# A hybrid attention/SSD/MoE block: the last gathers of expert rows without addition in the DMA, the addition on DVE

## Chip, cores and metric

One core of a Trainium2 chip runs the whole program. The metric is device time in microseconds, from the program's start to its end; lower is better. Beside it stands the span, from the first to the last instruction of a profiled execution.

## What is computed

One layer of a streaming encoder with 512 tokens of width 1024, in float32. What matters here is its last part:

```python
h1 = layernorm(alpha * h + mix)                       # mix: attention and SSD branches
moe = hier_moe(h1)                                    # 32 experts, 2 for each token, D_FF 256
ple = sigmoid(h1 @ w_ple_gate + b) * (p @ w_ple)
out = layernorm(alpha * h1 + moe + ple)
```

Each token picks one of 4 groups and in it 2 of 8 experts. An expert computes `silu(t @ w_gate) * (t @ w_up)`, weighted, times `w_down`. So the expert part of a token is the sum of two rows of 1024 numbers, one from each of its experts.

## The kernel before

**Tiling.** The 512 tokens are NT = 4 tiles of 128 partitions. The residual `alpha * h1 + ple` stands in SBUF as `base[:, i, :]`, one 128x1024 tile for each i, and is complete before the expert pairs begin (`s_base_ready` counts its 16 parts, all written by DVE). SBUF is one large array in two parts: the `ring` of 12 slots of 2048 words per partition, which holds weights, and the `arena` for all else. All code of a queue is written out by hand, one block for each engine: `sp` (weight loads), `pool` (GpSimd), `pe` (TensorE), `act` (ScalarE), `dve` (VectorE). Each engine works through its own list in order; semaphores tie the lists together.

**Experts.** The 32 experts run as PAIRS = 16 pairs, with room for CAP = 64 tokens for each expert, so a pair has 128 rows. Pair p uses the slots 6 (p mod 2) to 6 (p mod 2) + 5 of the ring: gate, up and down of the first expert, then of the second. For each pair TensorE multiplies gate and up (L1119, signal `s_gu_mm`), ACT takes the tanh (L1413), DVE forms the product in two instructions (L1981 and L1984 or L1986, in `hidden`), TensorE transposes it (L1144), multiplies down (L1134), and the 128x1024 result is copied out of PSUM in two halves, one by ACT and one by DVE (L2012, in `out_half`), into `eout`.

**Pairs 0 to 14.** POOL stores the rows of each pair by an indirect DMA (L754) to the tensor `y_rows` in HBM, which has a row for each place of each expert. Rows that no token takes are skipped. The semaphores `y_st[0]` and `y_st[1]` count the stores.

**The gathers.** Behind the 15 stores, POOL waits for both `y_st` and then issues eight indirect DMAs (L764). Gather (c, i) fetches for each token of tile i the row of its c-th choice (`rowsU`), and adds it to `base[:, i, :]` in the DMA (`compute_op=ALU.add`). All c = 0 come first, then c = 1; the gather (1, i) waits for the landing of (0, i), since both change the same tile. `y_gath[i]` counts the landings.

**Extra pairs.** Experts with over 64 tokens get extra pairs. Their number is known only at run time: each engine loads it from the tensor `ctl` (`value_load`, L2030 on DVE, L1449 on ACT) and runs a loop of MORE_PAIRS = 8 rounds with a branch in each (L2031 and L2032 on DVE, L1450 on ACT). In this data the number is zero, so the rounds do nothing.

**The last pair.** Pair 15 isn't stored. After the loop, TensorE combines its rows into each tile by a matmul with the matrix `last_rowsT`, tile by tile (L1157, in `combine`, 4 matmul records for each tile), to two PSUM banks that tiles i and i + 2 share: tiles 2 and 3 wait for `s_last_added`. Its input is `eout`, of which ACT and DVE copied a half each. DVE then waits for `y_gath[i]` = 32 and adds the banks to `base` (L2005, in `added`).

**The tail.** ACT takes the LayerNorm statistics of tiles 0 and 1, DVE those of tiles 2 and 3 (L1514 and L1515, in `tile_stats`), each behind the add of its tile. DVE then forms the roots for all tiles (L1519 to L1521), normalizes tiles 0 to 2 (L1523, L1524); ACT and POOL (L694, L695, `last_normed`) normalize tile 3; four DMAs write the output.

DVE's list around the change is, in order: `hidden(14)`, the row weights of the last pair (L1991 to L1999), `out_half` of pair 14, `hidden(15)`, the load and the loop, `out_half` of pair 15, then for each tile the wait, the add and the statistics.

Of the kernel before, what the change touches and what calls it, by code (L numbers as in the profile page):

```python
# [17 lines left out]
ALU = mybir.AluOpType  # L18
# [7 lines left out]
P = 128  # L26
D = 1024
S = 512
NT = S // P
# [211 lines left out]
def block_kernel(nc, aps, out):  # L241
    with ExitStack() as ctx:
# [154 lines left out]
        s_av_read = sem("av_read")  # L397
        s_ah1_ready = sem("ah1_ready")
        s_base_ready = sem("base_ready")
        s_bple_in = sem("bple_in")  # L400
        s_cb_act = sem("cb_act")
        s_cb_dve = sem("cb_dve")
# [99 lines left out]
        s_w_lo = sem("w_lo")  # L502
        s_wdt_split = sem("wdt_split")
        s_hT_hi = sem("hT_hi")
        s_wple_in = sem("wple_in")
        s_wsmall_in = sem("wsmall_in")
        s_xT_mm = sem("xT_mm")
        s_xdec_ready = sem("xdec_ready")
# [10 lines left out]
        s_yo_read = sem("yo_read")  # L519
        s_ys_read = sem("ys_read")  # L520
        s_z_read = sem("z_read")
        s_zero_set = sem("zero_set")
        s_zeroed = sem("zeroed")
        sems = {x.name: x for x in (
            s_av_read, s_dtT_read, s_cb_act, s_cb_dve, s_conv_read, s_dt_read, s_g_read, s_h1T_read, s_h_ready, s_hT_read, s_xgT_sb,
# [43 lines left out]
        def expert_slot_in(eng, former, parity, half, w):  # L569

            s = expert_slot(parity, half, w)
            eng.wait_ge(slot_in[s], former * 16 + 16 * (landings(s, len(loads) - 1) + 1))

        block = ctx.enter_context(nc.Block())

# [2 lines left out]
        def _(sp):  # L578
# [49 lines left out]
            sp.wait_ge(s_ys_read, KD)  # L628
            gate_slice(0)
            sp.wait_ge(s_pe_mix, 2 * NT)  # L630
            sp.dma_start(wple, aps["w_ple"][0].rearrange("(k p) n -> p k n", p=P)).then_inc(s_wple_in, 16)
            experts(0)
            sp.wait_ge(s_pe_pl, NT)
            gate_slice(2)
# [7 lines left out]
            with sp.Fori(0, MORE_PAIRS) as j:  # L642
                with sp.If(pairs > j):
                    sp.wait_ge(s_y_mm, j + LAST)
                    for half in range(2):
                        e = sp.value_load(ctl[0:1, bass.ds(j * 2 + half, 1)], min_val=0, max_val=NE - 1)
                        for w, t in ((0, wg), (1, wu)):
                            src = t[bass.ds(e, 1)].rearrange("a (p k) f -> p (a k) f", p=P)
                            slot = expert_slot(0, half, w)
                            sp.dma_start(ring[:, slot], src).then_inc(slot_in[slot], 16)  # L650
                        src = wd[bass.ds(e, 1)].rearrange("a (p k) n -> p (a k) n", p=P)
                        slot = expert_slot(0, half, 2)
                        sp.dma_start(ringN[:, slot], src).then_inc(slot_in[slot], 16)
                sp.nop()
# [3 lines left out]
        def _(pool):  # L658
# [26 lines left out]

            zt = shaped(R_Y, "p (r n) -> p r n", r=2, n=D)
            pool.wait_ge(s_dist_in, 1)
            g.memset(zt, 0.0).then_inc(s_zero_set, 1)
            pool.wait_ge(s_zero_set, 1)

            def last_normed(x, w, b, norms):

# [63 lines left out]
                    in_offset=None, bounds_check=ROWS - 1, oob_is_err=False).then_inc(y_st[p % 2], 16)  # L756
            for parity in range(2):
                pool.wait_ge(y_st[parity], 16 * (PAIRS // 2 - parity))
            pool.wait_ge(s_base_ready, 4 * NT)
            for c in range(2):  # L760
                for i in range(NT):
                    if c:
                        pool.wait_ge(y_gath[i], 16)
                    g.indirect_dma_start(  # L764
                        out=base[:, i, :], out_offset=None, in_=y_dram,
                        in_offset=bass.IndirectOffsetOnAxis(ap=rowsU[:, 2 * i + c:2 * i + c + 1], axis=0),
                        bounds_check=ROWS - 1, oob_is_err=True, compute_op=ALU.add).then_inc(y_gath[i], 16)
            pool.wait_ge(s_ln_in, 64)
            last_normed(base[:, NT - 1, :], A1w, A1b, 1)

# [2 lines left out]
        def _(pe):  # L773
# [289 lines left out]
            route(logits, NT - 1).then_inc(s_pe_rt, 1)  # L1063


            pe.wait_ge(s_wple_in, 16)
            pe.wait_ge(s_pT_read, 2)
            for n in range(4 * NT):
                s, i = divmod(n, NT)
# [406 lines left out]
        def _(dve):  # L1476
# [524 lines left out]
            def added(i, made, signal):  # L2001
# [3 lines left out]
                v.tensor_tensor(base[:, i, :], base[:, i, :], psum[:, b0:b0 + 2, :].rearrange("p b n -> p (b n)"), ALU.add)\  # L2005
                    .then_inc(signal, 1)

            def out_half(made, stores, u, signal):
                dve.wait_ge(*made)
                if not (isinstance(stores, int) and stores == 0):  # L2010
                    dve.wait_ge(y_st[u % 2], stores)
                v.tensor_copy(eout[:, u % 2, 512:1024], psum[:, 5, :]).then_inc(signal, 1)  # L2012

            dve.wait_ge(s_w_row, 16 * 2 * NT + 16)
            for p in range(PAIRS):
# [11 lines left out]
                    v.tensor_copy(rv[11], rv[8]).then_inc(s_more_added, 1)  # L2027
                out_half((s_y_mm, p + 1), 16 * q, p % 2, s_y_dve)

            pairs = dve.value_load(ctl[0:1, EXTRA + 1:EXTRA + 2], min_val=0, max_val=MORE_PAIRS)  # L2030
            with dve.Fori(0, MORE_PAIRS) as j:  # L2031
                with dve.If(pairs > j):  # L2032
                    dve.wait_ge(s_more_added, j * 4 + 1)
                    dve.wait_ge(s_rowf_moved, j + PAIRS // 2)
                    rows_weighted(more_rows, 0, j * 2 + 2, s_more_rows)
                    dve.wait_ge(s_more_rows, j * 3 + 1)
                    tokens_rows(j + PAIRS // 2, 0, j * 4 + 2 * PAIRS, j + PAIRS // 2, 2 * CAP)
                    hidden(j + PAIRS, 0)
                    out_half((s_y_mm, j + LAST + 1), 16 * (PAIRS // 2), 0, s_y_dve)
                    for i in range(NT):  # L2040
                        dve.wait_ge(y_gath[i], 32)
                        added(i, (s_more_mm, j * 4 + i + 1), s_more_added)
                dve.nop()

            out_half((s_last_y, 1), 16 * (LAST // 2), LAST % 2, s_last_y)
            for i in range(NT):
                dve.wait_ge(y_gath[i], 32)
                added(i, (s_last_mm, i + 1), s_last_added)
                if i >= 2:
                    dve.wait_ge(s_last_added, i + 1)  # L2050
                    tile_stats(base[:, i, :], i)
# [29 lines left out]
```

## Time and profile before

| | |
|---|---|
| median of 3 runs | 848.09 us (846.92 to 849.23) |
| the profiled execution: its own time | 849.05 us |
| its span, first to last instruction | 847.3 us |
| TensorE busy | 796.1 us, 94% of the span |
| DVE, ACT, POOL busy | 431.7, 176.2, 160.6 us |
| HBM read, written | 147.12 MB, 22.56 MB |
| mean granted TensorE clock | 0.981 of full |

All rows are of one profiled execution, in us from the span's start. A timeline row reads: start, duration, engine, line, operation, output from input, count, and in brackets the idle time of the engine ahead of it and what ended it. A chain row reads: start, duration, what; a DMA in it runs from its issue to the semaphore that released the next step. PEld is TensorE's weight load. A name with q (DVEq) is the sequencer of an engine, whose instructions (loads of a register, branches) count as no busy time.

### The profile page before, as it was taken

To read this page: it belongs to the slowest core of one execution; us is meant where nothing else is said; L and a number is where in the kernel's file an instruction comes from. 1 tells how busy PE (TensorE), PEld (TensorE's weight loads), DVE (VectorE), ACT (ScalarE), POOL (GpSimd) and SP (SyncE) were. 2 spreads that over 40 slices of the span, in tenths; PEclk is the share of its full clock that TensorE was granted. 3 is DMA by queue.
4 is the path that set the end of the run, shared out by engine and by line. 5 is a ranking of instruction groups with operands and counts; after the bars stand their busy time and mean duration, and the time that the engine had idled before them with its cause. 6 is when DMAs were issued, how large, how long until landed. Compare 5 with 4: busy or idle time off the path is not lost.

```text
span 847.3 us, 10153 instructions
## 1 busy us (share of the span) xinstructions
PE 796.1 (94%) x4045; PEld 534.1 (63%) x4045; DVE 431.7 (51%) x765; ACT 176.2 (21%) x327; POOL 160.6 (19%) x101
## 2 busy tenths in 40 slices
PE   5999999999999999999999999999999999998753
PEld 2987789998878787444444788884545454554221
DVE  6698765767688885112147579262313222301217
ACT  4213325553322230000000200221112111111012
POOL 4924760000323221000000344000000000000052
PEclk9999999999999999999999989999999999999886
DMA  9796331111311224613100631906999999999693
GB/s 302 294 368 143 100 98 52 51 51 51 98 51 51 50 51 142 255 50 100 50 0 1 261 137 51 347 1 268 420 422 421 421 420 424 419 422 423 286 178 120
DMA packets 58920, 166.25 MB, mean 196 GB/s; under 512 B 15813, under 2 KB 38495, under 8 KB 45050
## 3 DMA queue, kind: packets, MB, share of 16 engines
q1 hardware_dynamic: 51748, 139.69, 43.6%
q0 software_dynamic: 6432, 23.77, 8.8%
q10 hardware_dynamic: 694, 2.14, 0.6%
q8 instruction: 33, 0.54, 0.3%
q14 instruction: 13, 0.11, 0.0%
HBM read 147.12 MB, written 22.56 MB: 200 GB/s over the span
## 4 chain that ended last, share of the span: by engine, by line
PE 79%; DMA 11%; DVE 7%; issue 1%; ACT 1%; POOL 1%; SPq 0%; DVEq 0%; POOLq 0%
PE psum L806 24%; PE psum L1119 11%; PE psum L1034 7%; PE psum L1024 6%; PE psum L1073 5%; DMA ring<-in_w_exp_up_dram 5%; PE psum L1134 5%; PE psum L1015 3%; PE psum L1096 3%; PE psum L1097 3%; DMA ring<-in_w_in_dram 3%; DMA arena<-y_rows,rowsU 2%; PE psum L964 2%; PE psum L984 1%; PE psum L1075 1%; PE psum L914 1%
## 5 line engine op out<-in xcount | busy, mean ns | idle before, releaser
L806 PE MATMUL psum<-ring_r 128*128 128x512 f32 (+1 forms) x832 | 214.1, 345 | 4.6 <-DVE arena_r L1533 1.7
L806 PEld LDWEIGHTS psum<-ring_r 128*128 128x128 f32 x832 | 145.1, 191 | 25.7 <-issue 4.4
L1234 ACT COPY arena<-psum 128x256 f32<-128x256 f32 (+4 forms) x104 | 58.4, 579 | 288.2 <-PE psum L1041 139.8
L1119 PE MATMUL psum<-ring,arena 128*64 128x512 f32 x512 | 112.8, 593 | 4.0 <-DMA ring<-in_w_exp_up_dram 3.2
L701 POOL TENSOR_TENSOR ring_r<-ring,ring_r 128x2048 fp32r<-128x2048 f32 x16 | 73.9, 4622 | 204.8 <-ACT ring_r L1234 204.8
L806 PE MATMUL psum<-arena_r,ring_r 128*128 128x512 f32 (+1 forms) x288 | 106.0, 368 | 0.0
L1119 PEld LDWEIGHTS psum<-ring,arena 128*64 128x64 f32 x512 | 38.1, 137 | 76.0 <-issue 75.0
L1981 DVE SCALAR_TENSOR_TENSOR arena<-arena,psum 128x256 f32<-128x256 f32 x16 | 10.0, 624 | 111.3 <-ACT arena L1413 111.3
L1096 PE MATMUL psum<-arena_r 128*128 128x256 f32 x256 | 65.3, 293 | 0.0
L1134 PE MATMUL psum<-ring,arena 128*64 128x512 f32 x256 | 62.2, 631 | 1.6 <-issue 1.6
L754 POOL DMA_INDIRECT y_rows<-arena,storeU x15 | 14.6, 975 | 258.7 <-DVE arena L2012 258.7
L1097 PE MATMUL psum<-arena_r 128*128 128x256 f32 x256 | 62.4, 282 | 0.0
L806 PEld LDWEIGHTS psum<-arena_r,ring_r 128*128 128x128 f32 x288 | 55.1, 191 | 8.3
L1073 PE MATMUL psum<-arena 128*128 128x256 f32 x256 | 59.3, 386 | 0.0
L1034 PE MATMUL psum<-ring,arena 128*128 128x512 f32 x128 | 55.2, 593 | 1.6 <-DVE arena L1801 1.6
L1096 PEld LDWEIGHTS psum<-arena_r 128*128 128x128 f32 x256 | 48.8, 191 | 11.4 <-issue 11.4
L1024 PE MATMUL psum<-arena,ring 128*128 128x512 f32 x128 | 55.1, 592 | 0.0
L1073 PEld LDWEIGHTS psum<-arena 128*128 128x128 f32 x256 | 49.5, 194 | 6.9
L2012 DVE COPY arena<-psum 128x512 f32<-128x512 f32 x16 | 11.1, 692 | 79.0 <-PE psum L1134 79.0
L1097 PEld LDWEIGHTS psum<-arena_r 128*128 128x128 f32 x256 | 48.9, 191 | 0.0
L1034 PEld LDWEIGHTS psum<-ring,arena 128*128 128x128 f32 x128 | 24.2, 190 | 32.5 <-issue 30.1
L1024 PEld LDWEIGHTS psum<-arena,ring 128*128 128x128 f32 x128 | 24.3, 190 | 30.6 <-issue 30.6
(265 smaller groups left out, 1004.6 us busy)
## 6 DMA issues: line engine op xcount, KB each, us to landing
ring<-in_w_exp_gate_dram SPq DMA_DIRECT2D x32, 1024.0 KB, 11.6
ring<-in_w_exp_up_dram SPq DMA_DIRECT2D x32, 1024.0 KB, 15.6
ring<-in_w_exp_down_dram SPq DMA_DIRECT2D x32, 1024.0 KB, 16.2
ring<-in_w_in_dram SPq DMA_DIRECT2D x18, 1024.0 KB, 5.3
y_rows<-arena POOLq DMA_DIRECT2D x12, 1024.0 KB, 16.9
ring<-in_w_out_ssd_dram SPq DMA_DIRECT2D x4, 1024.0 KB, 7.2
ring<-in_w_out_dram SPq DMA_DIRECT2D x4, 1024.0 KB, 18.5
arena<-in_w_ple_gate_dram SPq DMA_DIRECT2D x4, 1024.0 KB, 7.9
```

The source lines that it names most:

```text
L701: g.tensor_tensor(lo, ring[:, SLOT_OF[seq]], hi.bitcast(F32), ALU.subtract).then_inc(s_w_lo, 1)
L806: t = mm(o, a, b, start=(first and j == 0), stop=(last and j == 2))
L964: t = mm(o[:, m * P:(m + 1) * P], dta[:, c, hh:hh + 1].broadcast_to([P, P]), upper, start=True, stop=True)
L1015: t = mm(o, ringN[:, s, j % 2, n * P:(n + 1) * P], yaT[:, j, :], start=(j == 0), stop=(j == 3))
L1024: t = mm(o, ringN[:, s, k % 2, n * P:(n + 1) * P], yT[:, :, k, :], start=(k == 0), stop=(k == KD - 1))
L1034: t = mm(o, mixT[:, k, i * P:(i + 1) * P], ringN[:, s, k % 2, b * 512:(b + 1) * 512], start=(k == 0), stop=(k == KD - 1))
L1073: mm(o[:, 0:PS], h1T[:, i, k, :], pgw[s % 2][:, k, :], start=(k == 0), stop=(k == KD - 1))
L1096: mm(o, h_hi[i][:, k, :], onehot[q % 2][:, i, 0:width], start=(i == 0), stop=False)
L1097: t = mm(o, h_lo[:, i, k, :], onehot[q % 2][:, i, 0:width], start=False, stop=(i == NT - 1))
L1119: t = mm(psum[sides[half], parity, :], xgT[buf][:, k, c:c + CAP], ring[:, s:s + 2, k, :], start=(k == 0), stop=(k == KD - 1))
L1134: t = mm(psum[sides[half], 4 + b, :], eactT[:, parity, k, sides[half]], ringN[:, s, k, b * 512:(b + 1) * 512], start=(k == 0), stop=(k == 1))
L1234: return nc.scalar.copy(dst, src)
```

## The change

The eight gathers drop the addition. Gather (c, i) writes to a free place of the ring, `back(i, c)`: half a slot for each tile, slots 0 and 1 for c = 0, slots 6 and 7 for c = 1. DVE adds it to `base[:, i, :]` by an instruction of its own (`back_added`, signal `s_back_added`): the four of c = 0 behind `hidden(15)` and ahead of the load and the loop over extra pairs, those of c = 1 behind the loop and `out_half`, each ahead of the add of its tile. POOL no longer waits for `s_base_ready` (DVE does); ahead of the gathers of c = 1 it waits for `s_gu_mm` = 16, as pair 15's gate and up are read from slots 6 and 7. Each gather (1, i) still waits for the landing of (0, i). In the loop over extra pairs, SP and DVE wait for the four adds. Two semaphores are dropped to make room: the load of `w_ple` is counted with other small loads, and the zeroing of a tile with POOL's own steps.

```diff
--- before.py
+++ after.py
@@ -397,6 +397,7 @@
         s_av_read = sem("av_read")
         s_ah1_ready = sem("ah1_ready")
         s_base_ready = sem("base_ready")
+        s_back_added = sem("back_added")
         s_bple_in = sem("bple_in")
         s_cb_act = sem("cb_act")
         s_cb_dve = sem("cb_dve")
@@ -502,7 +503,6 @@
         s_w_lo = sem("w_lo")
         s_wdt_split = sem("wdt_split")
         s_hT_hi = sem("hT_hi")
-        s_wple_in = sem("wple_in")
         s_wsmall_in = sem("wsmall_in")
         s_xT_mm = sem("xT_mm")
         s_xdec_ready = sem("xdec_ready")
@@ -519,7 +519,6 @@
         s_yo_read = sem("yo_read")
         s_ys_read = sem("ys_read")
         s_z_read = sem("z_read")
-        s_zero_set = sem("zero_set")
         s_zeroed = sem("zeroed")
         sems = {x.name: x for x in (
             s_av_read, s_dtT_read, s_cb_act, s_cb_dve, s_conv_read, s_dt_read, s_g_read, s_h1T_read, s_h_ready, s_hT_read, s_xgT_sb,
@@ -570,6 +569,10 @@
 
             s = expert_slot(parity, half, w)
             eng.wait_ge(slot_in[s], former * 16 + 16 * (landings(s, len(loads) - 1) + 1))
+
+        def back(i, c):
+
+            return ringN[:, 6 * c + i // 2, i % 2, :]
 
         block = ctx.enter_context(nc.Block())
 
@@ -628,7 +631,7 @@
             sp.wait_ge(s_ys_read, KD)
             gate_slice(0)
             sp.wait_ge(s_pe_mix, 2 * NT)
-            sp.dma_start(wple, aps["w_ple"][0].rearrange("(k p) n -> p k n", p=P)).then_inc(s_wple_in, 16)
+            sp.dma_start(wple, aps["w_ple"][0].rearrange("(k p) n -> p k n", p=P)).then_inc(s_wsmall_in, 16)
             experts(0)
             sp.wait_ge(s_pe_pl, NT)
             gate_slice(2)
@@ -642,6 +645,7 @@
             with sp.Fori(0, MORE_PAIRS) as j:
                 with sp.If(pairs > j):
                     sp.wait_ge(s_y_mm, j + LAST)
+                    sp.wait_ge(s_back_added, NT)
                     for half in range(2):
                         e = sp.value_load(ctl[0:1, bass.ds(j * 2 + half, 1)], min_val=0, max_val=NE - 1)
                         for w, t in ((0, wg), (1, wu)):
@@ -685,8 +689,7 @@
 
             zt = shaped(R_Y, "p (r n) -> p r n", r=2, n=D)
             pool.wait_ge(s_dist_in, 1)
-            g.memset(zt, 0.0).then_inc(s_zero_set, 1)
-            pool.wait_ge(s_zero_set, 1)
+            link(g.memset(zt, 0.0))
 
             def last_normed(x, w, b, norms):
 
@@ -756,15 +759,16 @@
                     in_offset=None, bounds_check=ROWS - 1, oob_is_err=False).then_inc(y_st[p % 2], 16)
             for parity in range(2):
                 pool.wait_ge(y_st[parity], 16 * (PAIRS // 2 - parity))
-            pool.wait_ge(s_base_ready, 4 * NT)
             for c in range(2):
+                if c:
+                    pool.wait_ge(s_gu_mm, PAIRS)
                 for i in range(NT):
                     if c:
                         pool.wait_ge(y_gath[i], 16)
                     g.indirect_dma_start(
-                        out=base[:, i, :], out_offset=None, in_=y_dram,
+                        out=back(i, c), out_offset=None, in_=y_dram,
                         in_offset=bass.IndirectOffsetOnAxis(ap=rowsU[:, 2 * i + c:2 * i + c + 1], axis=0),
-                        bounds_check=ROWS - 1, oob_is_err=True, compute_op=ALU.add).then_inc(y_gath[i], 16)
+                        bounds_check=ROWS - 1, oob_is_err=True).then_inc(y_gath[i], 16)
             pool.wait_ge(s_ln_in, 64)
             last_normed(base[:, NT - 1, :], A1w, A1b, 1)
 
@@ -1063,7 +1067,7 @@
             route(logits, NT - 1).then_inc(s_pe_rt, 1)
 
 
-            pe.wait_ge(s_wple_in, 16)
+            pe.wait_ge(s_wsmall_in, 16 * 4)
             pe.wait_ge(s_pT_read, 2)
             for n in range(4 * NT):
                 s, i = divmod(n, NT)
@@ -2005,6 +2009,13 @@
                 v.tensor_tensor(base[:, i, :], base[:, i, :], psum[:, b0:b0 + 2, :].rearrange("p b n -> p (b n)"), ALU.add)\
                     .then_inc(signal, 1)
 
+            def back_added(i, c):
+
+                dve.wait_ge(y_gath[i], 16 * c + 16)
+                if c:
+                    dve.wait_ge(s_back_added, i + 1)
+                v.tensor_tensor(base[:, i, :], base[:, i, :], back(i, c), ALU.add).then_inc(s_back_added, 1)
+
             def out_half(made, stores, u, signal):
                 dve.wait_ge(*made)
                 if not (isinstance(stores, int) and stores == 0):
@@ -2027,6 +2038,9 @@
                     v.tensor_copy(rv[11], rv[8]).then_inc(s_more_added, 1)
                 out_half((s_y_mm, p + 1), 16 * q, p % 2, s_y_dve)
 
+            dve.wait_ge(s_base_ready, 4 * NT)
+            for i in range(NT):
+                back_added(i, 0)
             pairs = dve.value_load(ctl[0:1, EXTRA + 1:EXTRA + 2], min_val=0, max_val=MORE_PAIRS)
             with dve.Fori(0, MORE_PAIRS) as j:
                 with dve.If(pairs > j):
@@ -2037,14 +2051,15 @@
                     tokens_rows(j + PAIRS // 2, 0, j * 4 + 2 * PAIRS, j + PAIRS // 2, 2 * CAP)
                     hidden(j + PAIRS, 0)
                     out_half((s_y_mm, j + LAST + 1), 16 * (PAIRS // 2), 0, s_y_dve)
+                    dve.wait_ge(s_back_added, NT)
                     for i in range(NT):
-                        dve.wait_ge(y_gath[i], 32)
                         added(i, (s_more_mm, j * 4 + i + 1), s_more_added)
                 dve.nop()
 
             out_half((s_last_y, 1), 16 * (LAST // 2), LAST % 2, s_last_y)
             for i in range(NT):
-                dve.wait_ge(y_gath[i], 32)
+                back_added(i, 1)
+                dve.wait_ge(s_back_added, NT + 1 + i)
                 added(i, (s_last_mm, i + 1), s_last_added)
                 if i >= 2:
                     dve.wait_ge(s_last_added, i + 1)
```

## Rows read from the trace of the kernel before

**Rows 1.** The page, its head, part 1 and part 5.

```profile
span 847.3 us, 10153 instructions
...
PE 796.1 (94%) x4045; PEld 534.1 (63%) x4045; DVE 431.7 (51%) x765; ACT 176.2 (21%) x327; POOL 160.6 (19%) x101
...
L1134 PE MATMUL psum<-ring,arena 128*64 128x512 f32 x256 | 62.2, 631 | 1.6 <-issue 1.6
```

**Rows 2.** The chain of waits, the last 50 us: start, us, what.

```profile
800.46 3.22 DMA y_rows<-arena,storeU
...
806.49 1.58 POOL arena L764
...
808.38 9.44 DMA arena<-y_rows,rowsU
...
818.56 9.20 DMA arena<-y_rows,rowsU
...
833.46 0.22 DVE arena L1515
```

**Rows 3.** Windows: length, busy time of each engine, then PEclk, DMA share, GB/s.

```profile
720.00:740.00 20.00, 20.00 (x109) 9.38 (x106) 5.62 (x8) 2.81 (x6) 1.38 (x2) 1.00 1.02 422
800.00:804.00 4.00, 4.00 (x22) 1.40 (x20) 0.00 (x0) 0.00 (x0) 0.97 (x1) 1.00 0.21 80
816.00:820.00 4.00, 3.22 (x9) 1.44 (x8) 0.69 (x1) 0.59 (x1) 1.44 (x1) 1.00 1.06 211
824.00:828.00 4.00, 3.90 (x6) 1.55 (x6) 1.48 (x3) 3.83 (x9) 0.00 (x0) 0.58 1.04 206
```

**Rows 4.** The timeline of the last 44 us, all engines.

```profile
804.50 1.68 POOL L764 DMA_INDIRECT arena<-y_rows,rowsU  x1 [3.07 <-DMA y_rows<-arena,storeU]
...
806.85 0.60 DVE L1986 TENSOR_TENSOR arena<-arena,psum 128x256 f32<-128x256 f32 x1
...
810.25 1.57 POOL L764 DMA_INDIRECT arena<-y_rows,rowsU  x1 [0.30 <-issue]
...
816.07 0.69 DVE L2012 COPY arena<-psum 128x512 f32<-128x512 f32 x1 [8.63 <-PE psum L1134]
...
816.82 3.70 PE L1157 MATMUL psum<-arena 128*128 128x512 f32 x8 [0.78 <-DVE arena L2012]
...
824.10 5.40 PE L1157 MATMUL psum<-arena 128*128 128x512 f32 x8 [3.58 <-DVE arena L2005]
...
829.05 1.42 DVE L1514 BATCH_NORM_STATS2 arena<-arena 128x6 f32<-128x512 f32 x2
...
830.75 1.22 DVE L2005 TENSOR_TENSOR arena<-arena,psum 128x1024 f32<-128x1024 f32 x1
...
832.00 1.42 DVE L1514 BATCH_NORM_STATS2 arena<-arena 128x6 f32<-128x512 f32 x2
```

**Rows 5.** Lines of the load and the loop, on DVE and ACT: ns min/median/max, starts.

```profile
L2030 DVEq TENSOR_LOAD <-ctl x1: 1740/1740/1740, 806.9 to 806.9; - x1
...
L2031 DVEq COMPARE_BRANCH  x8: 50/56/72, 809.8 to 814.7; - x8
...
L1449 ACTq TENSOR_LOAD <-ctl x1: 478/478/478, 805.8 to 805.8; - x1
...
L1450 ACTq COMPARE_BRANCH  x8: 40/45/55, 807.0 to 810.0; - x8
```

**Rows 6.** The timeline of POOL and of DVE, indirect stores beside adds.

```profile
518.45 1.81 POOL L743 DMA_INDIRECT row_weights<-arena,rowsU  x1 [0.30 <-issue]
520.56 0.98 POOL L743 DMA_INDIRECT row_weights<-arena,rowsU  x1 [0.30 <-issue]
521.85 0.98 POOL L743 DMA_INDIRECT row_weights<-arena,rowsU  x1 [0.30 <-issue]
...
518.18 1.23 DVE L1949 TENSOR_TENSOR arena_r<-arena 128x1024 fp32r<-128x1024 f32 x1
...
520.57 1.24 DVE L1952 TENSOR_TENSOR arena_r<-arena_r,arena 128x1024 fp32r<-128x1024 f32 x1
```

## The prediction

> **What bounds the kernel now.** I read the page's first part, then the chain of waits for the last 50 us, then the timeline of that stretch, the sources of a few lines and windows. TensorE is busy 94% of the span [rows 1], but the change touches nothing ahead of the last pair, and there the chain has left TensorE: the store of pair 14's rows, then gathers, then DVE [rows 2]. The store is released 3.22 us after its issue; the two longest links are gathers of 9.44 and 9.20 us; DVE ends its work on the last tile at 833.67, and what follows (roots, norms, output) takes 13.6 us and is not touched. The eight adding gathers keep all 16 DMA engines busy at 211 GB/s, where weight loads get 422 GB/s at the same share [rows 3]: an adding gather costs twice the engine time of its bytes, 524 KB / 211 = 2.5 us each, 20 us in all. So now the tail is bound by the DMA engines. One thing more lies in it, which matters below. Between its last work on pair 15 (the product issued at 806.85) and the copy of its output half at 816.07 [rows 4], DVE loads the number of extra pairs and runs the empty loop over them: the load starts at 806.9 and takes 1.74 us, the last branch is at 814.7 [rows 5]. The half copy came 1.3 us after that, so today the loop hides behind pair 15 on TensorE and ACT, with 1.3 us to spare.
>
> **The change, part by part.**
> *Gathers made plain.* With no addition in the DMA I expect the rate of a plain transfer, 524/422 = 1.24 us each. The trace has no plain gather of rows; its issue on POOL is bounded by the indirect stores of weights (0.98 us, start to start 1.29 [rows 6]) and by the adding gathers (1.57, and 1.89 from the start at 806.49 to that at 808.38 [rows 2]). I take 1.29: the stores are the only plain form, and the adding one has to read its target as well. The first gather stays at 804.50, since its wait (both parities of stores) is unchanged. The fourth then starts at 804.50 + 3 x 1.29 = 808.4. Landing: the store moved 80 GB/s x 4 us = 320 KB [rows 3] in 3.22 us; the gather moves 204 KB more, 0.5 us, so 3.7 us, and the fourth lands at **812.1**. The second four are issued at 809.7 to 813.5, their new wait (TensorE done with pair 15's gate and up) already over, since ACT has taken up that result before its own load at 805.8 [rows 5]; all land by 817.5. Where DVE's part below is right, nobody waits for them.
>
> *The second four, added on DVE.* Four more instructions of 128x1024 with both inputs in SBUF, 1.22 to 1.24 us [rows 6].
>
> *The first four, added on DVE ahead of the loop.* This is the term that decides. They stand behind the product of 806.85 and before the load. In the time from 807.45 to 816.07 DVE has 8.6 us without work, so 4 x 1.25 = 5 us look free; but the engine's queue is in order, and the load and the loop now start only when the fourth add is issued, which waits for the fourth gather. From the issue of the instruction ahead of the load to the end of the loop took 814.75 - 806.85 = 7.9 us, and some 0.05 us more to the next instruction. Whether the load waits for the instruction ahead to end isn't shown: that add is 0.6 us longer than the product of now. I take 0.25 of it. So the half copy comes at 812.1 + 7.95 + 0.25 = **820.3** in place of 816.07. TensorE's combination of the last pair needs both halves of that output, and waits with it; behind it in DVE's queue stands the whole list of the tail.
>
> *From the half copy to the end of the statistics.* Now: 833.67 - 816.07 = 17.6 us, of which much is waiting for gathers. After: copy and start of TensorE 0.75; the combination of tile 0, 1.85 us at the full clock (8 matmuls in 3.70) or 2.4 at half (824.10 and on) [rows 4]. TensorE will have been idle for 4.9 us; in the trace its granted clock was 0.58 of full in the window 824 to 828 [rows 3], after 3.58 us without work [rows 4], so I take 2.4, less than an even half because part of it ran at full. DVE's add of tile 0's gathered rows hides beside it. Then the add of tile 0 from PSUM 1.25, three tiles of two adds each 3 x 2.5 = 7.5, and two statistics of 1.68 (829.05 to 830.75, and 832.00 to 833.67) 3.35. Sum 0.75 + 2.4 + 1.25 + 7.5 + 3.35 = 15.25, against 17.6. TensorE's later combinations (tile 2 after the add of tile 0) stay ahead of DVE, and so do ACT's statistics of two tiles, which start with the adds of tiles 0 and 1, and TensorE's rows for the last norm, behind its combination of tile 3.
>
> *The rest costs nothing.* The two dropped semaphores wait for the same events; POOL's wait for the finished residual goes to DVE, which wrote it itself ahead of the expert pairs; SP's new wait stands in the loop over extra pairs, which is empty (L1134, the down matmuls, ran 256 times, 16 for each of 16 pairs [rows 1]). POOL's list behind the gathers (last norm) waits for ACT as now. Slots 0, 1, 6 and 7 of the ring are read by nobody after pair 15's gate and up.
>
> **Sum.** 820.3 + 15.25 = 835.55, against 833.67: +1.9 us. The gain of 2.35 us in the second stretch is more than paid for by 4.2 us of delay ahead of it. The profiled execution took 849.05 (span 847.3), the median is 848.09; the difference is put on the median: **850.0 us**, +0.2%. A measurement of this kernel can tell about 0.3% (2.5 us) from no change, so the forecast is "within".
>
> **A rule against the trace.** On contention between the new adds and POOL: in rows 6 an issue that began at 518.45 beside a two-input DVE instruction took 1.81 us in place of 0.98, while the next, which began together with another such, took 0.98, and the DVE instructions kept their 1.22 to 1.24. If each of the last four issues lost 0.83, the last would land near 820.8, and DVE asks for it after 830: no effect. The Trainium skill (SBUF — State Buffer, "SBUF: two separate sides") says that DVE and GpSimd share a port pair as an exclusive lock, held for a whole instruction, taken by a DVE instruction with two SBUF inputs only against a GpSimd instruction that reads SBUF. That rule would speak against the change if the lock worked the other way too: the rival E.
>
> For the landing, the Trainium skill (DMA: Bandwidth & Descriptors, "Anatomy of one DMA — SWDGE (gpsimd) path") gives a fit of 2.0 us and bytes over 436 GB/s, an estimate of 3.2 us for this gather. By it the sum would be +1.4; my 3.7 is the trace's store lengthened.
>
> **The rivals.**
> A, the forecast: 850.0, itself between +1.1 (clock full, load not waiting) and +3.0 (load waits for the whole add, a straggling engine lands the gather 0.7 later).
> B, slower: the plain gathers keep POOL for 1.57 us. The fourth is then issued at 810.25 as now and lands 0.6 us later after its issue: 814.55, the half copy is at 822.8, and the end moves by +4.4: 852.5. It passes the bound of 0.3% once the fourth gather lands after 812.7, that is from a spacing of about 1.45 us. For it: the duration could belong to the gather's direction, not to the addition. Against: the plain stores at 0.98.
> C, the load or the loop is shorter when moved. ACT's load took 0.48 beside DVE's 1.74, and its loop ends at 810.1 after 3.5 us beside DVE's 5.8 [rows 5]. Should the load have been held by POOL's issue (which ended at 808.07 [rows 2], the load at 808.6), it may be 1.2 shorter; then 848.5. With the loop at ACT's pace instead, 847.7; with both, 846.2.
> D, faster: the half copy isn't delayed at all (the load and loop run ahead of the waiting adds, or finish by 816). Then the clock has no idle stretch to fall in, 816.07 + 14.7 = 830.8, -2.9 us: 845.2. It is the most the change can give, as DVE's own list of 14.7 us then bounds; and it needs a landing by 808, against the 3.7 us.
> E, POOL's issue holds up the fourth add by up to 0.98 us: +2.9, 851.0. In rows 6 no DVE instruction did that.
>
> **How the numbers follow.** A 0.57, of which 0.15 lies over the bound of 2.5 us (landing and load both late); B 0.25; C 0.10; D 0.05; E 0.03. Faster 0.05 (D); within 0.42 + 0.10 = 0.52; slower 0.15 + 0.25 + 0.03 = 0.43. The range leaves out D and the end of C below, and the upper part of B: 847.3 to 852.9.
>
> **What would show it.** Right: DMA engines free between gathers, at no more than 1.3 us of full rate each; gathers 1.3 us apart; a wait of DVE for the fourth gather till about 812; the load's start at 812.1 and the loop's last branch at 820; the half copy at 820.3 with "issue" before it; TensorE's combination waiting for it since 816; no wait of DVE for a gather after that. Wrong: a half copy at 816 (then D), gathers 1.9 apart (B), a load of 0.5 us (C), or a wait in DVE's last list for a landing of the second four.

## The result

The changed kernel took **852.40 us** in the median of 8 runs (848.81 to 854.62), the kernel before 847.73 in 8 runs (846.03 to 849.23). The ratio is 1.0051 with a 95% interval of 1.003 to 1.0072. That is slower by half a per cent, 4.3 us by the ratio. The same two kernels on another chip gave 1.0053 (1.0031 to 1.0076).

The profiled executions hide this: the span after is 847.7 us beside 847.3 before. The one that was profiled after is also among the quickest of its kernel (849.49 beside the median of 852.40). What hides the rest lies ahead of the changed code: this execution came to the last pair's row weights 2.3 us earlier (786.62 in place of 788.93), and in the windows from 788 to 796 us its granted clock was 0.66 and 0.91 of full, where that of before was 0.82 and 0.50. So gate and up of pair 15, the last thing that both kernels do alike, ended at 805.75 before and at 802.28 after. From there on the stretches can be compared. The end of DVE's statistics came 27.9 us later before (833.67) and 31.9 us later after (834.15), so the tail is 3.9 us longer. The two ends of gate and up, and in the kernel before ACT's half copy, which began together with DVE's:

```profile
798.72 7.03 PE L1119 MATMUL psum<-ring,arena 128*64 128x512 f32 x32
...
816.07 0.59 ACT L1234 COPY arena<-psum 128x512 f32<-128x512 f32 x1 [5.59 <-PE psum L1134]
```

```profile
795.68 6.60 PE L1123 MATMUL psum<-ring,arena 128*64 128x512 f32 x30
```

First the chain of waits of the changed kernel (start, us, what), from the fourth gather to the first add from PSUM. L768 is the gather (L764 before), L2017 the add of gathered rows, L2044 to L2046 the load and the loop (L2030 to L2032), L2023 the half copy (L2012), L1161 the combination (L1157), L2009 the add from PSUM (L2005).

```profile
805.09 5.67 DMA ring<-y_rows,rowsU
...
810.78 0.56 DVE arena L2017
...
811.37 0.21 DVEq L2044
...
817.33 0.05 DVEq L2045
...
817.49 0.70 DVE arena L2023
...
818.24 6.29 PE psum L1161 x8
```

The chain of before [rows 2] had nothing of DVE's sequencer in it; now 5.7 us of the tail (from the loop's first move at 811.69 to its last branch at 817.33) are an empty loop, and the 0.9 us ahead of it, from the issue of the fourth add at 810.78, are the load. The timeline of the same stretch shows both sides of it:

```profile
801.03 1.09 POOL L768 DMA_INDIRECT ring<-y_rows,rowsU  x1 [3.06 <-DMA y_rows<-arena,storeU]
...
803.38 0.60 DVE L1990 TENSOR_TENSOR arena<-arena,psum 128x256 f32<-128x256 f32 x1
...
805.09 1.01 POOL L768 DMA_INDIRECT ring<-y_rows,rowsU  x1 [0.30 <-issue]
...
805.48 1.22 DVE L2017 TENSOR_TENSOR arena<-arena,ring 128x1024 f32<-128x1024 f32 x1 [1.50 <-DMA ring<-y_rows,rowsU]
...
810.78 1.23 DVE L2017 TENSOR_TENSOR arena<-arena,ring 128x1024 f32<-128x1024 f32 x1 [0.19 <-DMA ring<-y_rows,rowsU]
...
813.86 0.58 ACT L1238 COPY arena<-psum 128x512 f32<-128x512 f32 x1 [6.85 <-PE psum L1138]
817.49 0.69 DVE L2023 COPY arena<-psum 128x512 f32<-128x512 f32 x1 [5.49 <-issue]
...
818.24 9.71 PE L1161 MATMUL psum<-arena 128*128 128x512 f32 x16 [4.41 <-DVE arena L2023]
...
822.13 1.22 DVE L2009 TENSOR_TENSOR arena<-arena,psum 128x1024 f32<-128x1024 f32 x1 [2.81 <-PE psum L1161]
...
833.93 0.21 DVE L1519 BATCH_NORM_AGGREGATE arena<-arena 128x2 f32<-128x12 f32 x1
```

ACT copies its half at 813.86, as soon as TensorE's down matmuls end. DVE's half, which before began at the same instant as ACT's (816.07), comes 3.6 us later, with "issue" as what ended its idle time. TensorE stood 4.41 us for it. Then DVE stood 2.81 us for TensorE. The last two facts hang together by the clock, in the windows of the changed kernel (columns as in rows 3):

```profile
804.00:808.00 4.00, 1.20 (x4) 0.53 (x6) 1.32 (x2) 0.37 (x1) 2.97 (x3) 0.80 0.92 298
808.00:812.00 4.00, 4.00 (x12) 1.35 (x10) 3.58 (x3) 0.00 (x0) 2.75 (x3) 0.50 0.94 343
818.20:822.10 3.90, 3.87 (x5) 1.80 (x6) 1.11 (x1) 0.00 (x0) 0.00 (x0) 0.50 0.00 0
```

The combination of tile 0 ran at 0.50 and took 3.9 us, 818.2 to 822.1. The DMA engines moved 298 to 343 GB/s, no longer the 211 of [rows 3], and were idle from 817 on. The rows of the load and the loop on DVE, to be read beside [rows 5]:

```profile
L2044 DVEq TENSOR_LOAD <-ctl x1: 546/546/546, 810.8 to 810.8; - x1
...
L2045 DVEq COMPARE_BRANCH  x8: 50/56/72, 812.5 to 817.3; - x8
```

### The profile page after: what moved, and what is told of

Read it like the earlier page. It is cut to its first block, busy times and chain, and to the rows that moved or that the text cites. A ratio compares the mean times of both kernels' runs of the same rounds, so it can differ in the third digit from the quotient of the medians.

```text
span 847.7 us, 10167 instructions
## 1 busy us (share of the span) xinstructions
PE 797.7 (94%) x4045; PEld 534.4 (63%) x4045; DVE 439.8 (52%) x773; ACT 176.1 (21%) x327; POOL 156.8 (18%) x101
## 4 chain that ended last, share of the span: by engine, by line
PE 79%; DMA 9%; DVE 7%; issue 2%; POOL 1%; ACT 1%; SPq 0%; DVEq 0%; POOLq 0%
PE psum L810 24%; PE psum L1123 11%; PE psum L1038 7%; PE psum L1028 6%; PE psum L1077 6%; DMA ring<-in_w_exp_up_dram 5%; PE psum L1138 5%; PE psum L1019 3%; PE psum L1100 3%; PE psum L1101 3%; DMA ring<-in_w_in_dram 2%; PE psum L968 2%; PE psum L988 1%; PE psum L1079 1%; PE psum L918 1%
## 5 line engine op out<-in xcount | busy, mean ns | idle before, releaser
L2023 DVE COPY arena<-psum 128x512 f32<-128x512 f32 x16 | 11.1, 691 | 74.7 <-PE psum L1138 69.3
```

## The experiments

My theory, Q, was the prediction's: the loop behind the waiting adds delays the half copy, and TensorE with it. Against it stood W (DVE merely has more work) and C (it is the clock). In the table all times are in the span of each profiled execution. The last column is the distance from the end of gate and up of pair 15 to the end of the statistics, which leaves out what differs ahead of it. The ratio is to the kernel before on the same chip, with its 95% interval.

| kernel | gate, up end | down end | half copy starts | statistics end | distance | ratio |
|---|---|---|---|---|---|---|
| before | 805.75 | 816.04 | 816.07 | 833.67 | 27.9 | 1 |
| changed | 802.28 | 813.82 | 817.49 | 834.15 | 31.9 | 1.0051 (1.003 to 1.0072) |
| e1 changed, again | 803.36 | 814.04 | 818.66 | 835.08 | 31.7 | 1.0053 (1.0031 to 1.0076) |
| e2 branch around DVE's loop | 806.64 | 816.92 | 817.04 | 831.80 | 25.2 | 0.998 (0.9963 to 0.9997) |
| e3 all adds late | 803.12 | 813.50 | 813.54 | 832.63 | 29.5 | 1.0026 (1.001 to 1.0043) |
| e4 ACT copies both halves | 803.16 | 814.71 | 815.2 (ACT) | 832.26 | 29.1 | 1.0027 (1.0011 to 1.0043) |
| e5 before, branch on DVE | 805.20 | 815.49 | 815.53 | 831.89 | 26.7 | 1.0005 (0.9983 to 1.0028) |
| e6 branch on three engines | 804.59 | 811.05 | 814.45 | 831.01 | 26.4 | 0.9986 (0.9969 to 1.0003) |
| e7 e6, ACT copies both | 803.36 | 811.22 | 811.7 (ACT) | 826.88 | 23.5 | 0.9956 (0.9936 to 0.9977) |
| e8 before, three branches | 804.96 | 812.82 | 812.86 | 832.07 | 27.1 | 1.001 (0.9992 to 1.0028) |
| e9 early adds on other data | 806.21 | 816.74 | 816.77 | 831.53 | 25.3 | 0.9977 (0.996 to 0.9994) |
| e10 second four held back | 801.90 | 813.46 | 817.08 | 833.77 | 31.9 | 1.0043 (1.0022 to 1.0064) |

**e1: the changed kernel again.** No edit.

> The changed kernel unchanged, as the common measure for the others. Theory Q (queue order: the load and the empty loop of DVE stand behind the four early adds, so DVE's half copy of the last pair comes 3 to 4 us after TensorE's down matmuls end, and TensorE idles behind it): the half copy starts 3.2 to 4.2 us after the end of the down matmuls, with issue as what ended the idle time. Rival W (work: DVE's list simply got longer by eight adds, 9.8 us): the same delay would be of no weight, the end of the statistics is set by the adds alone. Rival C (clock: the loss is TensorE's granted clock, which falls while it waits): the combination of the last pair runs at half clock for most of its 16 matmuls. Time 849 to 854.

Measured: median 850.95. The half copy came 4.6 us after the down matmuls' end, a little over what was expected. The two executions agree in their distance to 0.2 us. It remains the common measure, with one caution: in the kernel before it isn't as steady, as e5 and e8 below show (26.7 and 27.1 in place of 27.9, at no gain in time). As Rival C asked, the combination of tile 0 ran at half clock here too (0.54 of full from 819.4 to 823.1).

**e2: one branch around DVE's empty loop.**

```diff
-            with dve.Fori(0, MORE_PAIRS) as j:
-                with dve.If(pairs > j):
+            with dve.If(pairs > 0):
+                with dve.Fori(0, MORE_PAIRS) as j:
+                    with dve.If(pairs > j):
...
```

> One branch around DVE's empty loop, so that behind the load of the count nothing is left of the 5.7 us of rounds. Theory Q: the load ends about 0.6 us after the issue of the fourth add, the half copy starts within 0.1 us of the end of the down matmuls, TensorE waits 0.8 us in place of 4.4, and the time falls by 3.5 to 5 us against the changed kernel, to 847 to 849, or just below the kernel before. Rival W: nothing changes, as all eight adds are still there. Rival C: gain only if the clock stays full in the combination.

Measured: median 845.05, 5.9 us below e1 on the same chip, where 3.5 to 5 were expected, and below the kernel before (0.998). Timeline of DVE:

```profile
815.48 1.23 DVE L2017 TENSOR_TENSOR arena<-arena,ring 128x1024 f32<-128x1024 f32 x1 [0.70 <-DMA ring<-y_rows,rowsU]
817.04 0.69 DVE L2023 COPY arena<-psum 128x512 f32<-128x512 f32 x1 [0.34 <-PE psum L1138]
...
819.88 1.22 DVE L2009 TENSOR_TENSOR arena<-arena,psum 128x1024 f32<-128x1024 f32 x1 [1.01 <-PE psum L1161]
```

and the windows of the combination:

```profile
817.70:821.50 3.80, 3.71 (x9) 1.78 (x10) 2.79 (x4) 0.36 (x1) 0.00 (x0) 1.00 0.71 268
```

All eight adds are there, the loop alone is gone, and with it more than the loss. The half copy waits for TensorE and no longer for issue; the combination ran at full clock and DVE stood 1.0 us for it in place of 2.8. The distance fell by 6.6 to 6.7 us: 3.6 to 4.5 of the half copy's delay, 1.7 to 1.8 for tile 0 of the combination at full clock, and the down matmuls, which in this execution ended 0.4 to 1.3 us sooner behind gate and up. The last item is no gain of the branch: the down matmuls took 5.35 us here, 5.74 in e1 and 6.61 in the first trace of the changed kernel, where the granted clock was 0.50 from 808 to 812. W is refuted. C is half true: the slow combination is a part of the loss, but it goes when the wait goes. In all the traces of kernels that have the new gathers, tile 0's combination ran at 0.50 to 0.54 of full where TensorE had waited 4.2 to 5.4 us for the copies (changed, e1, e6, e10), and at full clock where it had waited 0.8 to 1.2 us (e2, e3, e4, e7, e9).

**e3: the four early adds behind the half copy.**

```diff
-            for i in range(NT):
-                back_added(i, 0)
             pairs = dve.value_load(ctl[0:1, EXTRA + 1:EXTRA + 2], min_val=0, max_val=MORE_PAIRS)
...
             for i in range(NT):
-                back_added(i, 1)
-                dve.wait_ge(s_back_added, NT + 1 + i)
+                for c in range(2):
+                    dve.wait_ge(y_gath[i], 16 * c + 16)
+                    if c:
+                        dve.wait_ge(s_back_added, 2 * i + 1)
+                    v.tensor_tensor(base[:, i, :], base[:, i, :], back(i, c), ALU.add).then_inc(s_back_added, 1)
+                dve.wait_ge(s_back_added, 2 * i + 2)
                 added(i, (s_last_mm, i + 1), s_last_added)
```

> All eight adds of gathered rows behind the half copy, none ahead of the load and loop. Theory Q: the half copy is at once behind the down matmuls, but DVE's list from there is 0.75 + 12 x 1.25 + 3.35 = 19.1 us, against 20.3 us from the end of the down matmuls to the end of the statistics in the changed kernel: 1 us less, 850 to 852. Rival W: the same time as the changed kernel within 0.5 us, or more. Rival C: the combination of tile 0 runs at full clock and TensorE is out of the way.

Measured: median 848.34, 2.6 us below e1, more than the 1 us expected. From the end of the down matmuls to the end of the statistics it took 19.1 us, as the list of instructions says. Doing the four adds late, with nothing to cover them, beats doing them early in a free stretch: a second blow to W.

```profile
804.22 0.60 DVE L1990 TENSOR_TENSOR arena<-arena,psum 128x256 f32<-128x256 f32 x1
813.54 0.69 DVE L2023 COPY arena<-psum 128x512 f32<-128x512 f32 x1 [8.72 <-PE psum L1138]
814.15 2.54 DVE L2063 TENSOR_TENSOR arena<-arena,ring 128x1024 f32<-128x1024 f32 x2
...
832.42 0.21 DVE L1519 BATCH_NORM_AGGREGATE arena<-arena 128x2 f32<-128x12 f32 x1
```

**e4: ACT copies both halves of the last pair.** The edit to ACT's list stands first, then that to DVE's.

```diff
             out_copy((s_last_y, 1), 16 * (LAST // 2), LAST % 2, s_last_y)
+            copy(eout[:, LAST % 2, 512:1024], psum[:, 5, :]).then_inc(s_last_y, 1)
...
-            out_half((s_last_y, 1), 16 * (LAST // 2), LAST % 2, s_last_y)
```

> ACT copies both halves of the last pair's output; DVE's early adds, load and loop stay as in the changed kernel. Theory Q: TensorE starts its combination 1.3 us after the down matmuls, in place of 4.4, while DVE is still in the loop; DVE goes from the end of the loop straight into its list (8 adds of 1.25 and 3.35 of statistics, 13.4 us), so the end of the statistics comes about 3 us earlier than in the changed kernel: 848 to 850. Rival W: 0.7 us less, the copy alone. Rival C: as Q, since TensorE's idle time is short and the combination is hidden behind DVE's loop anyway.

Measured: median 848.63, 2.3 us below e1; the distance fell by 2.6 to 2.8. The timeline shows TensorE released and DVE still held by the loop, to 819.08:

```profile
814.75 1.07 ACT L1238 COPY arena<-psum 128x512 f32<-128x512 f32 x2 [6.85 <-PE psum L1138]
815.87 3.70 PE L1161 MATMUL psum<-arena 128*128 128x512 f32 x8 [1.16 <-ACT arena L1238]
819.08 1.23 DVE L2018 TENSOR_TENSOR arena<-arena,ring 128x1024 f32<-128x1024 f32 x1 [5.48 <-issue]
```

So of the 6.6 us that e2 gains, about 2.7 go with TensorE's wait, its clock and the copy, and the other 3.9 remain while DVE's own list starts late. The split is rough: that list started 15.9 us after the end of gate and up here, against 15.2 and 15.3 in the two traces of the changed kernel, since the gathers landed later.

**e5 and e8: the branches in the kernel before.** e5 has e2's edit, e8 the same on TensorE and ACT too.

> The kernel before, with one branch around DVE's empty loop. Theory Q: no change from the kernel before (within 0.5 us), as its loop ended 1.3 us ahead of the half copy and its tail waits for the adding gathers anyway; so the gain of this branch in the changed kernel is a debt of the change, not a gain to be had before. Rival G (the loop costs in itself, wherever it stands): 2 us or more faster. DVE's load of the count took 1.74 us here beside an adding gather's issue and 0.55 in the changed kernel; if the adding issue is what holds it, it takes 1.7 again.

> The kernel before with a branch around the empty loop on all three engines. Theory Q: the down matmuls end 2.2 us earlier, but the eight adding gathers, bound by the DMA engines, still land one each 2.5 us until 828, and DVE's last adds wait for them: no change, or 0.3 us. Rival G: 2 us faster, and then the branches alone are worth more than the change.

Measured: 1.0005 (0.9983 to 1.0028) and 1.001 (0.9992 to 1.0028), no change in either, though the medians alone, 848.59 and 847.54 beside 846.06, look slower. That rules out G's 2 us. In e8 the half copy came 7.9 us after the end of gate and up in place of 10.3, and most of these 2.4 us (1.6, as the distance fell by only 0.8) were lost again in the wait for the adding gathers, 7.48 us in the second row of e8's timeline below. The windows of e8 behind it show the DMA engines full at 205 to 210 GB/s.

```profile
812.86 0.69 DVE L2014 COPY arena<-psum 128x512 f32<-128x512 f32 x1 [6.20 <-PE psum L1134]
821.03 1.22 DVE L2007 TENSOR_TENSOR arena<-arena,psum 128x1024 f32<-128x1024 f32 x1 [7.48 <-DMA arena<-y_rows,rowsU]
```

```profile
816.00:820.00 4.00, 1.30 (x4) 0.24 (x2) 0.00 (x0) 0.00 (x0) 2.31 (x2) 1.00 1.05 205
820.00:824.00 4.00, 1.70 (x2) 0.84 (x3) 1.71 (x2) 1.65 (x5) 0.82 (x1) 0.61 1.06 210
```

The loop cost nothing before that these intervals could show; the change made it cost. DVE's load of the count took 1.72 us in e5, beside an adding gather's issue, as before:

```profile
L2030 DVEq TENSOR_LOAD <-ctl x1: 1715/1715/1715, 806.3 to 806.3; - x1
```

**e6: branches on three engines in the changed kernel; e7: and ACT copies both halves.** The edits of e2 (on `pe`, `act`, `dve`) and of e4 together.

> The changed kernel with one branch around the empty loop on TensorE, ACT and DVE. TensorE's transpose of pair 15 then starts with DVE's product and not 1.2 us after it, ACT's copy 1 us earlier: the down matmuls would end 2.2 us earlier. Theory Q: little of it is gained beyond the branch on DVE alone, 0 to 1 us, since DVE stands at the fourth gather's landing, which now ends later than the down matmuls, and the half copy waits for it. Rival W: 2 us less than with the branch on DVE alone. 844 to 845.

> As the one with three branches, and ACT copies both halves of the last pair's output, so TensorE doesn't depend on DVE's place in its list. Theory Q: DVE goes from the fourth early add (end about 10 us after the gate and up matmuls) straight on: eight adds and two statistics, 13.4 us, so the end of the statistics comes 23.5 us after the end of gate and up, against 25.2 with the branch on DVE alone, 31.8 in the changed kernel and 27.9 before: 843 to 844, 0.3 to 0.4% below the kernel before. Rival C: the granted clock takes part of it back.

Measured: e6 846.03 (0.9986), e7 **842.50** (0.9956, 0.9936 to 0.9977, against a before of 846.06). In e6 the down matmuls ended at 811.05, 6.5 us after gate and up, but the fourth add stood in front of the half copy until 814.1, TensorE waited 4.2 us again, and its clock fell again, as the waits and the windows of e6 show:

```profile
PE psum L1161 <- DVE arena L2025: 4.2, 1, 4.2
...
DVE arena L2011 <- PE psum L1161: 2.8, 1, 2.8
```

```profile
815.20:819.10 3.90, 3.90 (x5) 1.83 (x6) 1.09 (x2) 0.00 (x0) 0.00 (x0) 0.50 0.78 271
```

The expectation of 844 to 845 was too good by 1 us: I had not counted the clock. e7 takes TensorE out of DVE's list, and its distance is the 23.5 us that was expected; the time came out slightly better than the 843 to 844 written down. Its chain shows what is left: the gather, the load and one branch, and DVE's list, with 2.0 us of TensorE's combination once in its place.

```profile
806.18 5.93 DMA ring<-y_rows,rowsU
...
812.14 0.56 DVE arena L2020
...
812.73 0.21 DVEq L2047
...
813.70 1.24 DVE arena L2020
...
816.24 2.00 PE psum L1161 x4
```

e7 beats both kernels: the one before by 0.4%, and the changed one by some 0.9% where the ratios of the two, taken on different chips, are set side by side (0.9956 and 1.0051).

**e9: the early adds wait for nothing.** They read a ring slot that no gather writes, so the kernel leaves the first four gathers out of the sum.

```diff
             for i in range(NT):
-                back_added(i, 0)
+                v.tensor_tensor(base[:, i, :], base[:, i, :], ringN[:, 2, i % 2, :], ALU.add).then_inc(s_back_added, 1)
```

> The four early adds keep their place and size, but read a ring slot that no gather writes, and so wait for none (the first four gathers are fetched and not added: that part of the sum is wrong data). Theory Q: the fourth add is issued 5.4 us after the end of gate and up in place of 8.5, the half copy comes 12.1 us after it in place of 15.2, near the end of the down matmuls, and the end of the statistics 27.5 in place of 31.8: 847 to 848, equal to the kernel before. Rival W: no gain, since the work is the same.

Measured: median 845.39 (0.9977), better than the 847 to 848 expected. Four adds of the same size at the same place delay nothing: the half copy waits for TensorE. The reason is not the one I wrote down:

```profile
807.31 0.60 DVE L1990 TENSOR_TENSOR arena<-arena,psum 128x256 f32<-128x256 f32 x1
807.76 4.60 DVE L2043 TENSOR_TENSOR arena<-arena,ring 128x1024 f32<-128x1024 f32 x4
816.77 0.69 DVE L2023 COPY arena<-psum 128x512 f32<-128x512 f32 x1 [4.41 <-PE psum L1138]
```

```profile
L2044 DVEq TENSOR_LOAD <-ctl x1: 543/543/543, 807.3 to 807.3; - x1
```

The load stands behind the four adds in the list, but it began at 807.3, before the first of them. Without a semaphore to wait for, DVE's sequencer handed all four adds on and went ahead into the load and the loop while the engine worked them off. So it isn't the adds ahead of the loop that delay it, but the wait in them. I had expected the load 5.4 us after the end of gate and up; it came after 1.1.

**e10: the second four gathers are held until the first four have landed.**

```diff
                 if c:
                     pool.wait_ge(s_gu_mm, PAIRS)
+                    for k in range(NT):
+                        pool.wait_ge(y_gath[k], 16)
```

> The gathers of the second four are issued only when all of the first four have landed. If the second four slow the landing of the fourth (5.7 us from its issue in place of the 3.7 forecast), it now lands 1 us or more earlier and the half copy with it: 0.5 to 1.5 us faster than the changed kernel. If the gathers move at this pace by themselves, the fourth lands as before and the time stays within 0.5 us, the second four still being in time for DVE.

Measured: 1.0043, a median of 851.08, within the intervals of the changed kernel. The fourth gather was issued at 804.71 and its add began at 810.38, 5.67 us later, as with the others in flight. That add also stood right behind the one before it; that the gather didn't land much earlier is seen on POOL, which waits for the same landing and issues its next gather only at 811.28. Timeline of POOL:

```profile
804.71 1.01 POOL L770 DMA_INDIRECT ring<-y_rows,rowsU  x1 [0.30 <-issue]
811.28 1.20 POOL L770 DMA_INDIRECT ring<-y_rows,rowsU  x1 [5.56 <-DMA ring<-y_rows,rowsU]
```

So the second four don't slow the first. It is the gathers' own pace.

## Why the prediction was right, and where it wasn't

The range held (852.40 lies in 847.3 to 852.9) and the mechanism is the one forecast. The likeliest case, "within 0.3%", is not what came: the case A came with more than its size, in the part beyond 2.5 us to which I had given 0.15. I had put that part down to a late landing and a late load; the landing was late, the load was not. Counted from the issue of the first gather, the statistics end 29.2 us later before and 33.1 after: +3.9, where +1.9 was forecast. The errors below make up the difference: +0.2 for the issues, +2.0 for the landing, -1.5 for the load, +1.4 for the combination. That the range held is in part luck: without the shorter load, which I hadn't forecast in A, the time would by this sum have passed the range's upper end.

- *Plain gathers at the plain form's issue.* Right. They took 1.01 to 1.09 us, start to start 1.39, 1.35 and 1.32; the fourth was issued 4.06 us after the first, forecast 3.9. B's spacing of 1.89 didn't come. (The bound that B names, a landing after 812.7, is a spacing of 1.49 by its own sum, not 1.45.)
- *The landing: mis-sized, +2.0.* "3.7 us" from issue to landing was 5.67. The step that failed is lengthening the store's 3.22 by its missing bytes at full rate. Already the first gather took 4.4 us (issue 801.03, add at 805.48), and gathers moved 298 to 343 GB/s and not 422. At 343 one needs 524/343 = 1.5 us, more than the 1.35 us between two issues, so each lands later after its own issue: the fourth was added 5.3 us after the first, though issued only 4.06 after it. The prediction priced the fourth as if it stood alone. By the Trainium skill's fit (DMA: Bandwidth & Descriptors, "Anatomy of one DMA — SWDGE (gpsimd) path") the estimate was 3.2; the first gather's 4.4 is 1.2 us above it, and the fourth's 5.67, which holds the queueing too, 2.5.
- *Load and loop behind the fourth add.* Right in its mechanism (e2, e3, e9), mis-sized by -1.5. From the issue of the fourth add to the half copy it took 6.7 us in place of 8.2: the load took 0.55 and not 1.74, and it didn't wait for the add, for which I had put 0.25. That is one half of rival C. (C's own figure of 848.5 takes 1.5 us off for a load shorter by 1.2; by 1.2 it is 848.8.) The loop's pace was unchanged: first move at 811.69, last branch at 817.33, 5.7 us. Whether the load waits for the add, which I had left open, is settled: it ended at 811.34, the add at 812.01.
- *The half copy* came 16.5 us after the first issue, forecast 15.8, the sum of these.
- *From the half copy to the statistics: mis-sized, +1.4.* 16.65 in place of 15.25. All of it is the combination of tile 0, 3.9 us where I took 2.4. The clock fell as forecast; I had taken the price from a stretch of before that ran only in part at half clock (0.62 of full from 824.1 to 826.5).
- *Nobody waits for the second four.* Right, also in e10. In e7 and e9, where DVE asks for them sooner, one add waits up to 0.4 us.
- *D, the half copy not delayed:* it needed the branch (e2) or adds that wait for nothing (e9). Its sum was right, a distance of 830.8 - 805.75 = 25.05 where e2 and e9 have 25.2 and 25.3, but its gain of 2.9 us was too high: the times fell by 1.7 and 1.9 us by their ratios. It was measured against the 27.9 of one execution, and e5 and e8 show 26.7 and 27.1 for a kernel that is as fast. With further edits (e7) 3.7 us were to be had.
- *E, POOL's issue holding up an add:* not seen, the adds took 1.22 or 1.23 in every run.

## What to carry to other kernels

A free stretch of an engine in the timeline is not free for an instruction that waits on a semaphore: what stands behind it in the list, loads of registers and empty loops included, stands still until the wait is over, while the same instruction without a wait cost nothing (four of them, in e9). Before such an instruction is put into a gap, count from its last wait on through all the sequencer's rows to the next thing that another engine needs. And a loop over a number that is mostly zero wants one branch around it: it was worth 5.9 us here once the change had put it on the path, and nothing that could be measured before.

## What the hardware showed that I had not expected

- DVE's register load took 1.74, 1.72 and 1.74 us (before, e5, e8), each beside the issue of an adding gather, and 0.54 to 0.55 in all kernels with plain gathers, beside a plain issue or (e10) beside none. What in the adding form holds it isn't shown.
- DVE's sequencer ran ahead of its engine by at least four instructions of 1.2 us (e9: the load began at 807.3, the last of the adds ended at 812.4).
- POOL's issues took longer beside DVE's adds with two inputs in SBUF. In e9, beside four in a row, two issues took 1.96 and 1.97 us and the others 1.01 to 1.09; in the changed kernel, with single adds, they took 1.01 to 1.37; in e3, without such adds beside them, 1.01 to 1.09. No case here put this on the path. That fits the exclusive lock of which the Trainium skill tells (SBUF — State Buffer, "SBUF: two separate sides"), for the direction in which DVE holds POOL; the section has the lock hold either way, which the prediction left open, and here no add of DVE was seen to be lengthened.

```profile
809.01 1.96 POOL L768 DMA_INDIRECT ring<-y_rows,rowsU  x1 [0.30 <-issue]
811.28 1.97 POOL L768 DMA_INDIRECT ring<-y_rows,rowsU  x1 [0.30 <-issue]
813.55 1.01 POOL L768 DMA_INDIRECT ring<-y_rows,rowsU  x1 [0.30 <-issue]
```

**Open.** Why plain row gathers move at 300 to 340 GB/s where weight loads reach 420, and why the first takes 4.4 us, was not tried. The changed kernel's times spread over 5.8 us, those of before over 3.2 in the same rounds, but over 5.5 to 6.6 on the three other chips. The length of the half-clock stretches varies from one execution to the next, but with one profile each this was not tied to the times.
